# The low parts of the delta layer's weights, subtracted on GpSimd instead of VectorE

## The reference, cut to what matters

```python
u = rms_norm(h, norm_g) @ w_in                       # 560 tokens x 2048, w_in 2048 x 12352
xp = concat([conv_prev, qkv]); c = silu(short_conv(xp, conv_w))          # 4 taps
q, k = l2_norm(c_q) * 128 ** -0.5, l2_norm(c_k);  v = c_v                # 16 q/k heads, 32 v heads
# chunks of 64 tokens, per head: solve (m + 1) sol = rhs, then a recurrence over the chunks
v_new = u - w @ S;  o = (q * exp(G)) @ S + (q k^T * decay) @ v_new;  S = S * exp(g_last) + k'^T v_new
o = rms_norm(o, out_norm_g) * silu(z);  h + o @ w_out
```

## Time and profile before

| what | value |
|---|---|
| median of 3 runs | 3767.62 us (3767.06 to 3768.44) |
| the profiled execution | 3772.53 us, span of its instructions 3770.7 us |
| busy: PE / DVE / ACT / POOL | 3585.5 / 2369.2 / 1406.5 / 6.0 us |
| the delta layer | about 104 to 2012 us of the span |
| one turn of the delta layer | 112.8 us |
| PE's granted clock, mean | 0.979 of full speed |

### The profile page before, as it was taken

How to read it: one execution, slowest core, us unless ns; L and a number is a source line. 1 busy time by engine, 2 the same in 40 slices (tenths; PEclk the granted TensorE clock), 3 DMA queues, 4 the chain that set the end, 5 groups by cost and what they waited for, 6 DMA issues and landing times. The chain is left out here.

```text
span 3770.7 us, 65365 instructions
## 1 busy us (share of the span) xinstructions
PE 3585.5 (95%) x26437; PEld 3400.3 (90%) x26437; DVE 2369.2 (63%) x4556; ACT 1406.5 (37%) x3003; POOL 6.0 (0%) x10
## 2 busy tenths in 40 slices
PE   5899999999999999999988999699999999999799
PEld 3899999999999999999888999499999999999699
DVE  4477887777887777887754222556556566565422
ACT  4334444444444444444433111233333333333322
POOL 0000000000000000000000000000000000000000
PEclk8999999999999999999999999899999999999899
DMA  3344333334342334342344333433342333332443
GB/s 111 99 101 103 90 93 87 86 86 103 91 99 82 88 82 103 92 101 82 85 135 147 109 108 94 108 99 93 87 113 85 98 99 88 110 89 80 125 125 98
DMA packets 698912, 372.61 MB, mean 99 GB/s; under 512 B 125043, under 2 KB 667110, under 8 KB 698054
## 3 DMA queue, kind: packets, MB, share of 16 engines
q1 hardware_dynamic: 605590, 294.81, 30.3%
q10 hardware_dynamic: 93024, 73.64, 6.3%
HBM read 311.11 MB, written 57.27 MB: 98 GB/s over the span
## 5 line engine op out<-in xcount | busy, mean ns | idle before, releaser
L878 PE MATMUL main<-xh,w_hi 128*128 128x280 f32 x3264 | 764.5, 316 | 23.9 <-DVE w_lo L1128 16.2
L878 PE MATMUL main<-xh,w_lo 128*128 128x280 f32 x3264 | 687.7, 292 | 0.0
L878 PE MATMUL main<-xl,w_hi 128*128 128x280 f32 x3264 | 686.8, 292 | 0.0
L878 PEld LDWEIGHTS main<-xh,w_hi 128*128 128x128 f32 x3264 | 521.4, 190 | 38.6 <-DVE w_lo L1128 20.5
L878 PEld LDWEIGHTS main<-xh,w_lo 128*128 128x128 f32 x3264 | 520.9, 189 | 0.0
L878 PEld LDWEIGHTS main<-xl,w_hi 128*128 128x128 f32 x3264 | 518.7, 189 | 0.0
L1934 PE MATMUL b_main<-xh,b_w_hi 128*128 128x272 f32 (+1 forms) x2048 | 459.2, 306 | 12.5 <-DVE b_w_lo L2141 12.5
L1934 PE MATMUL b_main<-xh,b_w_lo 128*128 128x272 f32 (+1 forms) x2048 | 430.0, 291 | 0.0
L1934 PE MATMUL b_main<-xl,b_w_hi 128*128 128x272 f32 (+1 forms) x2048 | 429.1, 291 | 0.0
L1934 PEld LDWEIGHTS b_main<-xh,b_w_hi 128*128 128x128 f32 x2048 | 325.9, 190 | 26.9 <-issue 12.6
L1934 PEld LDWEIGHTS b_main<-xh,b_w_lo 128*128 128x128 f32 x2048 | 327.0, 190 | 0.0
(11 more groups left out here) (291 smaller groups left out, 6229.9 us busy)
## 6 DMA issues: line engine op xcount, KB each, us to landing
w_raw<-in_a_w_in SPq DMA_DIRECT2D x192, 512.0 KB, 4.3
b_w_raw<-in_kv_w SPq DMA_DIRECT2D x64, 512.0 KB, 4.2
b_w_raw<-in_b_w_in SPq DMA_DIRECT2D x64, 512.0 KB, 4.1
a_w_raw<-in_a_w_out SPq DMA_DIRECT2D x52, 512.0 KB, 4.1
y_w_raw<-in_b_w_out SPq DMA_DIRECT2D x32, 512.0 KB, 5.6
M<-MT SPq DMA_DIRECT2D x16, 640.0 KB, 3.7
TT<-XT SPq DMA_DIRECT2D x16, 640.0 KB, 4.8
o<-ot ACTq DMA_DIRECT2D x16, 560.0 KB, 4.8
```

Source lines behind the costliest of these rows:

```text
L878: m = nc.tensor.matmul(main[2 * (t % 2) + h][:, 0:HALF], hi[:, n % SPLIT_RING, k, :], x[:, KSUB * (n % 2) + k, h * HALF:(h + 1) * HALF], s ...
```

## The change

The body of the "split" step moves from DVE's list to GpSimd's. GpSimd now walks through the same turns, and for each "split" waits for `hi_made` and makes the subtraction; the semaphores and the slots are the same.

```diff
             nc.gpsimd.memset(xp[:], 0.0).then_inc(ready, 1)
+
+            def body(turn):
+                for step in turn.steps():
+                    what, *a = step
+                    if what == "split":
+                        n, = a
+                        pool.wait_ge(hi_made, SUBS * turn.p + n + 1)
+                        nc.gpsimd.tensor_tensor(w_lo[:, n % SPLIT_RING], w_raw[:, n % RAW_RING],
+                                                w_hi[:, n % SPLIT_RING].bitcast(F32), ALU.subtract).then_inc(lo_made, 1)
+            turns(pool, body)
...
-                    if what == "split":
-                        n, = a
-                        dve.wait_ge(hi_made, SUBS * p + n + 1)
-                        nc.vector.tensor_tensor(w_lo[:, n % SPLIT_RING], w_raw[:, n % RAW_RING],
-                                                w_hi[:, n % SPLIT_RING].bitcast(F32), ALU.subtract).then_inc(lo_made, 1)
-                    elif what == "osplit":
+                    if what == "osplit":
```

## The result

The changed kernel takes 3842.62 us (median of 4 runs, 3841.26 to 3850.8) where the kernel before takes 3767.34 (4 runs): a ratio of 1.0207, 95% interval [1.0189, 1.0225], so 75 us slower. 3833 was forecast. The execution profiled after took 3841.26 us, of which 3839.5 are span, 68.8 more than before.

What follows compares the result with a forecast made beforehand. PE was taken to bound the layer. Blocking at 3.9 us a turn over 15 turns (59 us) plus 5.7 at the start gave 65 us, so 3833 us against the median, range 3757 to 3885.

Steps and rivals of the forecast that it cites:

- the three waits: PE's waits for the third sub-block's low part (0.37 us), `bv` in "sumsq" (0.36) and `on` in "otr" (0.22) would go.
- GpSimd's duration: One subtraction on GpSimd takes 2.2 us, between ends of 0.96 and 2.68, in time for PE.
- The start: At the layer's start, PE's first matmul comes 5.7 us later, paid once, range 1.7 to 6.0.
- The load of GpSimd's code: Before GpSimd's first subtraction, loading its code takes 4 us, between 0 and 4.3.
- "kqn" to "kkq": Subtractions hold `kqk` by 1.03 us and the last "decay" operation by 2.01; PE's third "kkq" group waits 2.5 us.
- "fsub": From "fsub" to "sumsq", subtractions hold the chain by 0.46 and 2.2 us; PE's wait in "sumsq" grows by 1.5.
- the seven at price 0: The other seven subtractions of a turn fall on taps with idle time behind, reciprocals or the recurrence: cost 0.
- "osq": A subtraction holds `on` from 972.91 to 973.23, costing PE 0.3 us a turn.
- The slow clock: A 1.2 GHz stretch behind PE's new wait each turn adds 26 us; kept only in the range.
- no collision: Rival: DVE's operations keep their durations beside GpSimd, so the kernel takes 3755 to 3759 us; chance 0.24.
- half speed: Rival: while both engines read, each goes at half pace, so the kernel takes 3778 us; chance 0.18.
- a subtraction of 2.85: Rival: blocking with subtractions of 2.85 us each, 6.8 us a turn, 3876 us; chance 0.10.

Runs made afterwards that it cites:

- the seven places: The changed kernel with only low parts 2 and 6 to 11 of each turn's twelve on GpSimd, the other five back on VectorE: 3757.49 us, ratio 0.9968.
- the one: The kernel before with only the third of the twelve low parts of a turn made on GpSimd: 3758.28 us, ratio 0.998.

## Why the prediction was right, point by point

The mechanism held: GpSimd's reads stop VectorE, and TensorE waits for it. That the sum lay so near is luck: errors of both signs met in it.

- *What bounds, and the gain.* TensorE bounds the layer, and VectorE's relief was worth almost nothing: shown by the seven places against the one. Of the three waits counted as a gain of 0.95 us a turn, the third sub-block's went and was worth about 0.7, twice what was booked; the two others came back in another form.
- *GpSimd's duration.* 2.2 forecast, 2.42 measured, between the value and the upper end. TensorE never waits for `w_lo` in a turn, as reckoned.
- *The start.* 5.7 us forecast, 1.6 measured (first matmul at 106.87 instead of 105.24). From the end of GpSimd's last fill to the first matmul it is 2.45 us instead of 0.55; the fill itself ended 0.27 us earlier in this execution. The load of GpSimd's code, put at 4, is not seen, as these rows of GpSimd show:

```profile
103.24 1.18 POOL L853 MEMSET xp<- 128x1296 f32 x1
104.47 4.67 POOL L861 TENSOR_TENSOR w_lo<-w_raw,w_hi 128x1024 fp32r<-128x1024 f32 x2
```

  The first subtraction starts 0.05 us behind the last fill, and the first two together take 4.67. The 6 us of the Trainium skill (GPSIMD Engine Reference, Instruction dispatch) are not on this path either; whether the load came earlier, hidden, stays open.
- *"kqn" to "kkq", 2.5 us forecast, none measured.* This step failed. The hold of `kqk` came as forecast (1.9 us longer). The second, on the last operation of "decay", did not: the forecast kept ACT's third high part at its old time, but on ACT it stands behind the exponential of `dec`, which waits for VectorE, and came 9.42 us into the turn instead of 8.70:

```profile
1130.97 0.74 ACT L1073 ACTIVATE dec<-dec 128x640 f32<-128x640 f32 x1 [2.37 <-DVE dec L1220]
1131.62 1.04 ACT L998 ACTIVATE w_hi<-w_raw 128x1024 fp32r<-128x1024 f32 x1
```
```profile
1131.81 0.82 DVE L1225 TENSOR_TENSOR bdec<-bdec,dec 128x640 f32<-128x640 f32 x1
```
```profile
1132.73 2.38 POOL L861 TENSOR_TENSOR w_lo<-w_raw,w_hi 128x1024 fp32r<-128x1024 f32 x1 [6.66 <-ACT w_hi L998]
```

  So a late VectorE delayed GpSimd's next start as well, past `bdec`'s end at 1132.63, if only by 0.1 us, and onto operations that read PSUM.
- *"fsub", 1.5 us in "sumsq" forecast, 3.2 in "knat" measured.* This step had the wrong place and was too small. "knat" needs the bank that the second `bv` reads, and this `bv` (892.63 before) stands ahead of the removed subtraction of 893.23, whose 1.13 us the forecast gave back first. Without them its own terms have that `bv` 0.46 + 2.2 = 2.7 us late, of which the 0.7 us between its end (893.32) and "knat" (894.03) would have taken part: a wait of about 2 us in "knat". Measured, `bv` is 3.6 us late. The 1.0 more: GpSimd's subtraction ended 0.6 us later in the turn than reckoned (25.66 us into it instead of 25.05), and it stopped `fsx`, which has a single SBUF input and was taken as free, so that `fsx` and the memset behind it still had to run, 0.4. The taps, which the forecast had among the seven at price 0, lost 2.0 us; the subtractions that were gone and the idle time there took that up, and nothing of them was left for `fsx` and the chain.
- *"osq", 0.3 forecast:* the wait for `on` grew from 0.22 to 0.68.
- *The slow clock, 26 us, left out of the value.* It came, and cost 24. The reason given for leaving it out was a shorter wait in "kkq"; the longer one in "knat" did the same.
- *The sum.* Forecast per turn 3.9, measured 2.9 at full clock, 43 us in fifteen turns instead of 59; start 1.6 instead of 5.7; clock 24 instead of 0. What is left, turn 0, turn 16 and the rest of the program, comes to about nothing. 65 was forecast and 69 came in the span. Of the rivals, no collision and half speed are refuted by `kqk`'s 3.41 us, and a subtraction of 2.85 by 2.42.

## What to carry to other kernels

Work moved to GpSimd is not taken off VectorE if both read SBUF: look, instruction by instruction, at what VectorE does during each GpSimd instruction, and move only those that fall on PSUM operations or slack. Here the price of a stop was what was left of GpSimd's instruction when VectorE's started, less 0.13 to 0.14 us: 1.93 of 2.07 for `kqk`, 1.79 of 1.92 for `fsx`, 2.13 of 2.27 for `fst`. One well placed subtraction of the twelve gave all that any of these kernels gained. When a delay is forecast in one place, let the other engines' lists move with it before pricing the next collision, and book a gain only where it comes ahead of the wait; and count the clock when a new idle stretch on a TensorE-bound path is as long as one that was followed by a slow stretch before.

## What was not expected of the hardware

A fill on GpSimd, which reads nothing, stops one-input operations of VectorE on SBUF (`fsx`, 380 to 1414 ns, and the first tap, 549 to 831) and leaves the two-input ones alone; a reading instruction stops both. A wait recorded as 0.37 us on TensorE was worth 0.7 us when it went. And 24 matmuls of no use in each turn made a kernel 32 us faster.
